# Expert up table read in pairs of neighbouring rows, gathers issued in order of release, and a third one-hot buffer, in a hybrid decoder layer

## The chip, the cores and the metric

The kernel runs on one core of a Trainium2 chip. The metric is the device time of one execution in microseconds (us); before the change it is 3395.63 us, the median of three runs (3392.81 to 3404.72).

## What is computed

One layer of a decoder for 1024 prompt tokens and 8 sample tokens, all in float32, with 1024 channels. Three gated branches (a convolution, windowed attention, attention to a memory) are summed and projected, and then comes a product-key expert mixer, which takes most of the time:

```python
q = (xb @ w_q).reshape(PEER_BLOCK, PEER_HEADS, 2, PEER_DK_HALF)
s = jnp.einsum('thcd,hcnd->thcn', q, keys)
sv, si = lax.top_k(s, PEER_TOPK)                       # 16 of 128 keys, twice per head
cand = sv[:, :, 0, :, None] + sv[:, :, 1, None, :]
cv, ci = lax.top_k(cand.reshape(...), PEER_TOPK)       # 16 of 256 pairs
eid = i0 * PEER_N_KEYS + i1                            # an expert is a pair of keys
u = w_down[eid]                                        # 128 experts per token
act = jax.nn.gelu(jnp.einsum('td,thkd->thk', xb, u), approximate=False)
out = jnp.einsum('thk,thkd->td', softmax(cv) * act, w_up[eid])
```

There are 16384 experts, so `w_down` and `w_up` are tables of 16384 rows of 4 KB (64 MB each). A token uses 128 of them.

## The kernel before, in words

**Tiles.** The tokens are cut into eight tiles of 128 (one token per partition) and the eight samples.

**Down side.** For each of the 1024 (tile, choice) pairs POOL issues one indirect DMA that gathers 128 rows of `w_down`, one per token, 512 KB in all (`fetch`, L1398), into one of a ring of row buffers; DVE multiplies it with the tokens and sums (`dot`, L2013, a "row" in what follows). The ring is a list of buffer places, each with a span of row numbers in which it may be used (`open_from`, `open_to`); from row 365 on a row's buffer is the one that was used five rows earlier, so five rows at most are on their way.

**Up side.** For the first seven tiles the sum over experts is a product with the whole table. PE scatters the 128 coefficients of each token into a dense 128 x 16384 matrix: DVE makes one-hot rows from the two key numbers (`one_hots`, L2037, four tokens for each compare, 32 compares a tile), ACT scales one of the two (`scaled`, L2315), PE multiplies them (`scatter`, L1463: "a scatter" is the product for four tokens), ACT copies the result out (`evacuate`, L2350). Then PE multiplies the dense matrix, in 128 blocks, with the table's blocks (`up_step`, L1660). SP reads a block of 512 KB (128 neighbouring rows, one for each partition) as one DMA (`fetch_up`, L1269) into one of four buffers; a block's DMA is issued once the step four blocks earlier has finished (`step_done`).

**Passes.** A stretch of 64 blocks is here called a pass, numbered 0 to 7. Pass n multiplies each block for tile n-1 (second half of its experts) and for tile n (first half), so that a block serves two tiles; pass 0 and pass 7 have one tile only. In the second half of passes 0 to 5 the 32 scatters of the next tile stand between the steps. The 32 scatters of tile 0 are woven between the last products ("items") ahead of pass 0. The last tile (tile 7) has no dense matrix: its 128 rows of `w_up` are gathered and added up on DVE (`up`, L2107).

**The order.** One list, `plan`, is made when the kernel is built, by a loop that simulates the engines with costs in a table and puts the next piece of DVE work down. DVE follows it word for word: rows, selections of keys and ids (the "keys" and "ids" entries, a pair of which makes one head), compares, sums. PE's order is fixed. Before the change POOL follows the same list: it issues the gathers of the rows up to the next "keys" entry, then waits until the head before is done and fetches that head's scores (`fetch_scores`, L1349), then the next rows.

## Time and profile before

| | before |
|---|---|
| median of three runs | 3395.63 us |
| profiled execution | 3393.68 us, of which 3391.9 us is the span that the profile shows |
| PE busy | 3106.5 us (92%) |
| DVE busy | 2512.9 us (74%) |
| DMA, mean over the span | 318 GB/s |
| granted TensorE clock, mean | 0.958 |

The profiled execution's time is 1.8 us more than its span, and 1.95 us less than the median. Windows of the trace (busy time of each engine between two times) cut the run into items (up to 1515 us), the eight passes (1515 to 3377 us) and the last normalisations. Shares of busy time say little here, since different engines set the pace in different stretches, so the waits of each stretch have to be read.

### The profile page before, as it was taken

The numbers are of one execution on the slowest core, as the hardware profiler recorded it, in microseconds if no ns is written. First come the engines' busy times: TensorE is split into PE (matmuls) and PEld (weight loads), VectorE is DVE, ScalarE is ACT, GpSimd is POOL, SyncE is SP. The second block draws the span as 40 slices with busy tenths as digits, with TensorE's granted clock in tenths as the row PEclk, the third lists the DMA queues.
The fourth block names the chain that finished last, engine by engine and source line by source line (L and its number), as shares of the span: only waits on it lengthen the run. The fifth ranks groups of instructions, "written<-read, shape, count | busy, mean of one in ns | idle before, by whom it ended". The sixth has DMA issues, their size and how long they took to land.

```text
span 3391.9 us, 33152 instructions
## 1 busy us (share of the span) xinstructions
PE 3106.5 (92%) x11349; PEld 1834.3 (54%) x11349; DVE 2512.9 (74%) x5082; ACT 779.3 (23%) x2062; POOL 1630.5 (48%) x1269
## 2 busy tenths in 40 slices
PE   8999798988888998778999999999999999997976
PEld 5677687857745754453545545545544545543322
DVE  2298435986877688878998888898888867646455
ACT  2001542312310003331503403403403403400000
POOL 0000002554055487862667656657756757644443
PEclk9999899999989799789999999999999999998999
DMA  3111457999398799999999999999999999899998
GB/s 131 44 36 65 151 194 252 336 365 333 129 342 313 296 401 379 340 336 345 388 393 393 355 376 366 359 389 381 356 389 369 351 399 377 321 411 393 408 410 328
DMA packets 326170, 1077.16 MB, mean 318 GB/s; under 512 B 40467, under 2 KB 73876, under 8 KB 325339
## 3 DMA queue, kind: packets, MB, share of 16 engines
q0 software_dynamic: 172416, 625.03, 48.1%
q1 hardware_dynamic: 119275, 428.87, 34.0%
q10 hardware_dynamic: 34312, 21.16, 2.0%
q8 instruction: 90, 1.47, 0.2%
q14 instruction: 77, 0.63, 0.1%
HBM read 1052.50 MB, written 23.94 MB: 317 GB/s over the span
## 4 chain that ended last, share of the span: by engine, by line
PE 37%; DMA 19%; DVE 14%; issue 10%; POOL 7%; ACT 1%; ACTq 0%; DVEq 0%; SPq 0%; POOLq 0%
PE psum L1660 22%; DMA arena<-in_w_down,arena 10%; DMA arena<-in_w_up,arena 7%; POOL arena L1398 6%; DVE arena L2013 5%; PE psum L1507 5%; PE psum L1463 4%; PE psum L1509 2%; PE psum L1636 1%; DMA arena<-in_w_q 1%; PE psum L1606 1%; DVE arena L2107 1%; DVE arena L2037 1%; DMA arena<-scratch_s 1%; PE psum L1523 1%
## 5 line engine op out<-in xcount | busy, mean ns | idle before, releaser
L1398 POOL DMA_INDIRECT arena<-in_w_down,arena x1024 | 1435.2, 1402 | 734.2 <-DVE arena L2013 484.9
L1660 PE MATMUL psum<-arena 128*128 128x512 f32 x3584 | 1603.8, 599 | 73.8 <-DMA arena<-in_w_up 70.4
L2013 DVE CUSTOM_DVE_ANT_0 arena<-arena 128x1024 f32<-128x1024 f32 x1024 | 1218.2, 1221 | 254.0 <-DMA arena<-in_w_down,arena 235.2
L1660 PEld LDWEIGHTS psum<-arena 128*128 128x128 f32 x3584 | 664.8, 192 | 869.6 <-issue 731.1
L1507 PE MATMUL psum<-arena 128*128 128x256 f32 (+2 forms) x1536 | 359.8, 388 | 16.1 <-DVE arena L1815 7.7
L2315 ACT ACTIVATE arena<-arena 128x128 f32<-128x128 f32 x896 | 286.1, 391 | 336.8 <-DVE arena L2037 317.5
L1463 PEld LDWEIGHTS psum<-arena 128*128 128x128 f32 x1792 | 244.3, 200 | 183.7 <-ACT arena L2315 104.3
L2037 DVE TENSOR_TENSOR arena<-constants,arena 128x1024 f32<-128x1024 f32 x224 | 273.4, 1222 | 88.0 <-PE psum L1463 72.9
L1507 PEld LDWEIGHTS psum<-arena 128*128 128x128 f32 x1536 | 266.4, 194 | 98.9 <-issue 15.5
L1463 PE MATMUL psum<-arena 128*128 128x128 f32 x1792 | 251.8, 286 | 71.7 <-ACT arena L2315 63.4
L2107 DVE SCALAR_TENSOR_TENSOR arena<-arena 128x1024 f32<-128x1024 f32 x128 | 164.4, 1284 | 133.1 <-DMA arena<-in_w_up,arena 130.8
L1349 POOL DMA_DIRECT2D arena<-scratch_s x64 | 37.6, 587 | 448.9 <-DMA scratch_s<-arena 214.6
L284 PE MATMUL psum<-arena 128*128 128x344 f32 x816 | 238.4, 455 | 3.0 <-DVE arena L324 3.0
L1398 POOL DMA_INDIRECT arena<-in_w_up,arena x128 | 130.0, 1016 | 170.7 <-DVE arena L2107 153.5
L2350 ACT ACTIVATE arena<-psum 128x128 f32<-128x128 f32 (+5 forms) x512 | 149.8, 352 | 265.4 <-PE psum L1463 210.6
L284 PEld LDWEIGHTS psum<-arena 128*128 128x128 f32 x816 | 155.7, 191 | 85.4 <-issue 5.7
L1509 PE MATMUL psum<-arena 128*128 128x256 f32 (+2 forms) x768 | 183.2, 381 | 0.0
L1335 POOL MEMSET constants<- 128x64 f32 x1 | 0.2, 152 | 346.5 <-POOLq L369 346.5
L345 DVE SCALAR_TENSOR_TENSOR arena<-arena,constants 128x1024 f32<-128x1024 f32 x120 | 154.2, 1285 | 4.3
L1636 PE MATMUL psum<-arena 128*128 128x256 f32 (+2 forms) x512 | 132.8, 422 | 23.6 <-DMA arena<-in_w_q 23.2
L1509 PEld LDWEIGHTS psum<-arena 128*128 128x128 f32 x768 | 132.8, 190 | 36.6 <-issue 0.3
L1636 PEld LDWEIGHTS psum<-arena 128*128 128x128 f32 x512 | 97.8, 214 | 54.5 <-DMA arena<-in_w_q 26.2
(317 smaller groups left out, 2078.5 us busy)
## 6 DMA issues: line engine op xcount, KB each, us to landing
arena<-in_w_up SPq DMA_DIRECT2D x512, 512.0 KB
arena<-in_w_gates SPq DMA_DIRECT2D x96, 768.0 KB
arena<-in_w_o SPq DMA_DIRECT2D x40, 512.0 KB
arena<-in_w_q SPq DMA_DIRECT2D x32, 512.0 KB
arena<-in_w_down,arena POOLq DMA_INDIRECT x1024
arena<-in_w_chunks SPq DMA_DIRECT2D x26, 512.0 KB, 3.4
arena<-scratch_s POOLq DMA_DIRECT2D x64, 128.0 KB
scratch_s<-arena ACTq DMA_DIRECT2D x11, 512.0 KB
```

The source lines that it names most:

```text
L284: mm = pe.matmul(psum[:, s + g, 0:GC], w[:, k, :], hT[:, k, g * GC:(g + 1) * GC], start=first, stop=last)
L345: link(dve.scalar_tensor_tensor(out=acc, in0=uT[:, c, t:t + SEQ], scalar=cw[:, c, t:t + 1], in1=acc, op0=ALU.mult, op1=ALU.add))
L1398: pool.indirect_dma_start(dst, None, table, bass.IndirectOffsetOnAxis(ap=idN[:, min(n, NT - 1) % 2, j:j + 1], axis=0)).then_inc(here, 16)
L1463: mm = pe.matmul(psum[:, 4 + g % 2, t * P:(t + 1) * P], pair[:, 1, t, :], pair[:, 0, t, :], start=True, stop=True)
L1507: pe.matmul(psum[:, b, 0:n], w[:, i, :], hT[:, i, cols], start=(i == 0), stop=(i == KD - 1))
L1509: mm = pe.matmul(psum[:, b + 1, 0:n], w[:, KD + c, :], branch[br][:, c, cols], start=(c == 0), stop=(c == NC - 1))
L1636: mm = pe.matmul(psum[:, b + h, 0:n], w[:, c, :], hT[:, c, cols], start=(c == 0), stop=(c == KD - 1))
L1660: mm = pe.matmul(psum[:, 2 * (m % 2) + h, :], coef_block(m, s % NKEYS), wup[s % WUPR][:, h * 512:(h + 1) * 512], start=first, stop=end)
L2013: dve.tensor_tensor_reduce(row, row, rowD[slot_of["x", n]], 1.0, 0.0, ALU.mult, ALU.add, dots[:, n % 3, j:j + 1]).then_inc(row_used, 1)
L2037: dve.tensor_tensor(out[:, g % 2], iota128.unsqueeze(1).unsqueeze(1).broadcast_to(full), ids[:, 0:2, BATCH * q:BATCH * (q + 1)].unsqueeze( ...
L2107: dve.scalar_tensor_tensor(out=acc, in0=row, scalar=dots[:, (NT - 1) % 3, u:u + 1], in1=acc if u else x1last, op0=ALU.mult, op1=ALU.add).t ...
L2315: ins = act.activation(buf[:, g % 2, 1, t, :], buf[:, g % 2, 1, t, :], ACT.Copy, scale=ids[:, 2, c:c + 1])
```

## The change

Four things are changed.

1. The up table is read in pairs: partition p gets the two neighbouring rows 128p + 2q and 128p + 2q + 1 (8 KB in one run), so a DMA moves 1 MB and there are 256 instead of 512. Partitions now lie 128 rows (512 KB) apart in the table. There are two buffers of 1 MB instead of four of 512 KB. A block is now "all experts with second key e" instead of "all with first key e", so the two operands of the scatter change places.
2. POOL has an order of its own, `pool_order`: row gathers, token tiles and score fetches are sorted by the time at which the plan's simulation has what each of them waits for.
3. Tile 0's one-hots have three buffers instead of two. The third stands where a row buffer (at 36864) was, which now closes at row 258 instead of 365.
4. The rule that places compares in the plan looks eight PE operations ahead instead of six for tile 0.

```diff
-        WUPR = 4
+        WUPR = 2
...
-            [310] + [258] * 2 + [50] * 2 + [238, 365]
+            [310] + [258] * 2 + [50] * 2 + [238, 258]
...
-        hot0 = at(33792, 2, 2, BATCH, P)
+        hot0 = [at(o, 2, BATCH, P) for o in (33792, 34816, 36864)]
+
+        def hot_of(g):
+            return hot0[g % 3] if g < NBATCH else hot[:, g % 2]
...
-        wup = [at(o, D) for o in (43008, 44032, 45056, 46144)]
+        wup = [at(43008 + 2 * D * i, 2, D) for i in range(WUPR)]
+        up_table = w_up.rearrange("(p e) d -> p e d", e=NKEYS)
...
-            if any(x[0:2] == ("scat", hot_next) for x in m.ops[m.at:m.at + (6 if hot_next < NBATCH else 1)]) and \
-                    m.done("turned", hot_next // NBATCH) and m.pe <= m.now + 6.5 and (hot_next < 2 or m.done("scated", hot_next - 2)):
+            if any(x[0:2] == ("scat", hot_next) for x in m.ops[m.at:m.at + (8 if hot_next < NBATCH else 1)]) and \
+                    m.done("turned", hot_next // NBATCH) and m.pe <= m.now + 6.5 and (hot_next < 3 or m.done("scated", hot_next - (3 if 2 < hot_next < NBATCH else 2))):
...
+        pool_order = [(m.fetch_at[f], 1, i, f) for i, f in enumerate(fetches)]
+        for k in range(HEADS * NT):
+            n, h = divmod(k, HEADS)
+            out_at = m.end["item", max(i for i in range(NI) if items[i] == ("score", n, h // 4))] + 5.0
+            pool_order.append((max(out_at, m.end["keys", (k - 1) // HEADS, (k - 1) % HEADS] if k else 0.0), 0, k, ("scores", n, h)))
+        for s in plan:
+            if s[0] in ("xprep", "sdown", "sup"):
+                pool_order.append((m.at_time[s], 2, 0, s))
+        pool_order = [x[3] for x in sorted(pool_order)]
...
-                def fetch_up(s):
-                    if s >= WUPR:
-                        sp.wait_ge(step_done, s - WUPR + 1)
-                    e = s % NKEYS
-                    sp.dma_start(wup[s % WUPR], w_up[e * NKEYS:(e + 1) * NKEYS, :])\
-                      .then_inc(wup_here[s % WUPR], 16)
+                def fetch_up(q):
+                    if q >= WUPR:
+                        sp.wait_ge(step_done, 2 * (q - WUPR + 1))
+                    e = 2 * q % NKEYS
+                    sp.dma_start(wup[q % WUPR], up_table[:, e:e + 2, :]).then_inc(wup_here[q % WUPR], 16)
...
-                for s in plan:
-                    if s[0] == "keys":
+                for s in pool_order:
+                    if s[0] == "scores":
                         fetch_scores(s[1], s[2])
-                    elif s[0] in ("dot", "up"):
-                        while fetched <= fetches.index(("row", row_index(s))):
-                            fetch(fetches[fetched])
-                            fetched += 1
+                    elif s[0] in ("row", "x"):
+                        fetch(s)
...
-                    if g >= 2:
-                        dve.wait_ge(scat_done, g - 1)
+                    if g >= (2 if n else 3):
+                        dve.wait_ge(scat_done, g - (1 if n else 2))
```

The plan's simulation then gives another order, so the change moves instructions on DVE and POOL. The first place is on DVE where tile 0's compares begin, among the last gated additions of the items (L1815 and L1818 before, L1826 and L1829 after). L2037 (L2048 after) is the compare, and each row's dot product is a pair of "ISA" entries at L2013 (L2024 after). Before:

```order
L1815 TENSOR_TENSOR arena<-arena,psum 128x392
L1818 TENSOR_TENSOR arena<-arena 128x3x128
L1818 TENSOR_TENSOR constants<-constants,arena 128x8
L2037 TENSOR_TENSOR arena<-constants,arena 128x1024 x2
L2013 ISA arena<-arena 128x1024
L2013 ISA arena 128x1
```

And after:

```order
L1826 TENSOR_TENSOR arena<-arena,psum 128x392
L1829 TENSOR_TENSOR arena<-arena 128x3x128
L1829 TENSOR_TENSOR constants<-constants,arena 128x8
L2048 TENSOR_TENSOR arena<-constants,arena 128x1024 x3
L2024 ISA arena<-arena 128x1024
L2024 ISA arena 128x1
```

Both stand after the same row; three compares instead of two now run ahead of the scatters. The second place is the 26th compare of tile 0 on DVE, in the middle of the woven scatters. L1973 to L1987 are the end of a head's selection. Before:

```order
L1973 MAX arena<-arena 128x8
L1975 TENSOR_TENSOR arena<-constants,arena 128x512
L1977 MAX arena<-arena 128x8
L1979 TENSOR_TENSOR arena<-arena 128x512
L1981 MAX_INDEX arena<-arena 128x8
L1983 TENSOR_REDUCE arena<-arena 128x2x16
L1985 MAX_INDEX arena<-arena 128x8
L1987 SCALAR_TENSOR_TENSOR arena<-arena 128x16
L2037 TENSOR_TENSOR arena<-constants,arena 128x1024
L2013 ISA arena<-arena 128x1024
```

And after, at the same compare (the last row):

```order
L2048 TENSOR_TENSOR arena<-constants,arena 128x1024
L2024 ISA arena<-arena 128x1024
L2024 ISA arena 128x1
L2024 ISA arena<-arena 128x1024
L2024 ISA arena 128x1
L2024 ISA arena<-arena 128x1024
L2024 ISA arena 128x1
L2024 ISA arena<-arena 128x1024
L2024 ISA arena 128x1
L2048 TENSOR_TENSOR arena<-constants,arena 128x1024
```

Before, three selection pieces stand between tile 0's first and last compare (10, 20 and 22 rows of the list, in all the keys of three heads and the ids of two); after, none does, and the first follows 19 rows after the 32nd compare. Counted in the whole lists, the rows (dot products) that DVE has ahead of some compares are: 32nd compare 371 before and 363 after; 64th 424 and 417; 96th 537 and 526; the last (224th) 983 and 971. The third place is the end of POOL's list. L1415 (L1426 after) are the eight gathers of `w_down` for the samples, which wait for the end of pass 5, L1421 (L1432) those of `w_up`. Before:

```order
L1392 DMA arena<-scratch_xn 128x1024
L1398 DMA arena<-in_w_down,arena 128x1024 x94
L1415 DMA arena<-in_w_down,constants 128x1024 x8
L1398 DMA arena<-in_w_down,arena 128x1024 x38
L1398 DMA arena<-in_w_up,arena 128x1024 x34
L1421 DMA arena<-in_w_up,constants 128x1024 x8
L1398 DMA arena<-in_w_up,arena 128x1024 x94
```

And after:

```order
L1406 DMA arena<-scratch_xn 128x1024
L1412 DMA arena<-in_w_down,arena 128x1024 x88
L1426 DMA arena<-in_w_down,constants 128x1024 x8
L1412 DMA arena<-in_w_down,arena 128x1024 x44
L1412 DMA arena<-in_w_up,arena 128x1024 x26
L1432 DMA arena<-in_w_up,constants 128x1024 x8
L1412 DMA arena<-in_w_up,arena 128x1024 x102
```

The samples' gathers, with their wait, stand after row 986 (1024 - 38) before and after row 980 (1024 - 44) now.

## Rows read from the trace of the kernel before

**Rows 1.** Window ahead of pass 0: busy us (x instructions), clock, DMA share, GB/s.

```profile
1300.00:1515.00 215.00, 164.90 (x672) 99.00 (x672) 183.79 (x333) 81.09 (x277) 163.38 (x109) 0.84 0.94 342
```

**Rows 2.** The same for passes 0 to 7: PE, PEld, DVE, ACT, POOL.

```profile
1515.00:1688.00 173.00, 149.25 (x516) 79.36 (x517) 154.21 (x390) 62.47 (x197) 74.17 (x57) 0.95 0.98 374
1688.00:1938.00 250.00, 250.00 (x772) 126.57 (x772) 218.30 (x479) 65.46 (x198) 171.52 (x123) 1.00 0.99 379
1938.00:2195.00 257.00, 251.79 (x772) 127.50 (x771) 224.09 (x511) 66.49 (x202) 160.44 (x119) 0.99 0.97 367
2195.00:2448.00 253.00, 249.59 (x773) 125.94 (x772) 221.41 (x491) 64.30 (x199) 171.09 (x121) 1.00 0.99 379
2448.00:2704.00 256.00, 250.15 (x771) 126.99 (x770) 218.76 (x492) 66.25 (x200) 170.41 (x121) 0.99 0.97 370
2704.00:2953.00 249.00, 249.00 (x775) 126.45 (x774) 182.36 (x287) 68.44 (x202) 152.23 (x107) 1.00 0.97 368
2953.00:3193.00 240.00, 222.52 (x512) 98.09 (x511) 122.55 (x155) 5.02 (x9) 112.42 (x109) 0.96 1.00 394
3193.00:3377.00 184.00, 142.01 (x289) 47.78 (x287) 102.70 (x81) 2.95 (x5) 73.90 (x73) 0.98 1.01 399
```

**Rows 3.** Chain that ended last, two neighbouring steps of pass 1: start us, us, what.

```profile
1803.70 3.44 PE psum L1660 x8
1808.03 3.44 PE psum L1660 x8
```

**Rows 4.** Waits of PE's weight loads, 1700 to 2953 us: us, times, longest.

```profile
PEld psum L1660 <- DMA arena<-in_w_up: 2.6, 2, 2.1
```

**Rows 5.** Waits of PE's weight loads, 3193 to 3377 us (pass 7).

```profile
PEld psum L1660 <- DMA arena<-in_w_up: 88.5, 58, 4.0
```

**Rows 6.** DMA queues, 3250 to 3350 us: packets, MB, share of 16 engines.

```profile
DMA packets 11244, 40.99 MB, mean 410 GB/s; under 512 B 1240, under 2 KB 1240, under 8 KB 11243
q0 software_dynamic: 5661, 20.61, 51.7%
q1 hardware_dynamic: 5582, 20.37, 50.9%
```

**Rows 7.** Windows of L1398 (gathers) on POOL, pass 1.

```profile
1688.00:1938.00 250.00, 166.62 (x114) 1.00 0.99 379
```

**Rows 8.** Windows of L2013 on DVE, pass 1 (two records for each row).

```profile
1688.00:1938.00 250.00, 133.36 (x224) 1.00 0.99 379
```

**Rows 9.** Waits of PE's weight loads, 1190 to 1515 us.

```profile
PEld psum L1463 <- ACT arena L2315: 44.5, 14, 8.4
```

**Rows 10.** Timeline of DVE, then of PE: start us, us, what [idle before <-releaser].

```profile
1314.39 0.29 DVE L1892 MAX8 arena<-arena 128x8 f32<-128x128 f32 x1
...
1316.74 1.21 DVE L2037 TENSOR_TENSOR arena<-constants,arena 128x1024 f32<-128x1024 f32 x1
...
1319.03 2.08 PE L1463 MATMUL psum<-arena 128*128 128x128 f32 x8 [5.33 <-ACT arena L2315]
```

**Rows 11.** Waits of DVE, 1190 to 1515 us.

```profile
DVE arena L2013 <- DMA arena<-in_w_down,arena: 35.6, 33, 4.1
```

**Rows 12.** DMA, issues with median us to landing.

```profile
arena<-in_w_chunks SPq DMA_DIRECT2D x26, 512.0 KB, 3.4
```

**Rows 13.** DMA, 3 to 9 us, when only reads of 8 KB runs (token matrix) move.

```profile
DMA packets 339, 2.53 MB, mean 422 GB/s; under 512 B 32, under 2 KB 32, under 8 KB 32
```

**Rows 14.** DMA queues, 640.95 to 643.6 us: gate weights (6 KB runs, q1) beside gathers (4 KB, q0).

```profile
q1 hardware_dynamic: 117, 0.68, 62.4%
q0 software_dynamic: 121, 0.42, 40.1%
```

**Rows 15.** Timeline of POOL at the samples' gathers.

```profile
2938.28 1.68 POOL L1398 DMA_INDIRECT arena<-in_w_down,arena  x1 [0.60 <-DVE arena L2013]
2958.43 0.94 POOL L1415 DMA_INDIRECT arena<-in_w_down,constants  x1 [18.48 <-PE psum L1660]
```

**Rows 16.** Windows, the end of pass 5.

```profile
2943.00:2960.00 17.00, 17.00 (x58) 8.95 (x57) 6.36 (x10) 7.15 (x15) 1.26 (x2) 1.00 0.51 144
```

More of the change, by code:

```diff
@@ L943, in ask_rows @@
                         return
-                    self.pool = max([self.pool, self.row_done.get(c - 1, 0.0)] + [self.end[x] for x in [needs] + joins])
+                    free = max([self.row_done.get(c - 1, 0.0)] + [self.end[x] for x in [needs] + joins])
+                    self.fetch_at[f] = max(free, self.fetch_at.get(fetches[self.next_fetch - 1], 0.0))
+                    self.pool = max(self.pool, free)
                     self.pool += 1.24 if f[0] == "row" else 0.3
@@ L1030, in put @@
                 self.now += 0.3 + group_cols(items[s[1]][3])[1] / 450.0 if s[0] == "evac" else COST[s[0]]
-                self.end[s] = self.now
+                self.end[s] = self.at_time[s] = self.now
             def done(self, *s):
@@ L1284, in _ @@
                 sp.wait_ge(xb_done, NX)
-                for s in range(WUPR - 1):
-                    fetch_up(s)
+                for q in range(WUPR - 1):
+                    fetch_up(q)
                 for i in range(2):
@@ L1290, in _ @@
                 sp.wait_ge(item_done, NI)
-                for s in range(WUPR - 1, HALF * (DENSE + 1)):
-                    fetch_up(s)
-                    k, i = s // HALF, s % HALF
+                for q in range(WUPR - 1, HALF * (DENSE + 1) // 2):
+                    fetch_up(q)
+                    k, i = 2 * q // HALF, 2 * q % HALF
                     if i == 40 and k == 1:
@@ L1455, in scatter @@
                     g = NBATCH * n + q
-                    pair = (hot if n else hot0)[:, g % 2]
+                    pair = hot_of(g)
                     pe.wait_ge(hot_ready, g + 1)
@@ L1660, in up_step @@
                         mm = pe.matmul(psum[:, 2 * (m % 2) + h, :], coef_block(m, s % NKEYS),
-                                       wup[s % WUPR][:, h * 512:(h + 1) * 512], start=first, stop=end)
+                                       wup[s // 2 % WUPR][:, s % 2, h * 512:(h + 1) * 512], start=first, stop=end)
                     return mm
                 def piece_here(s):
-                    pe.wait_ge(wup_here[s % WUPR], 16 * (s // WUPR + 1))
+                    pe.wait_ge(wup_here[s // 2 % WUPR], 16 * (s // 2 // WUPR + 1))
                 pe.wait_ge(copied, len(copy_no))
```

21 lines of the change are left out of this document (9 added, 12 removed).

## The prediction, made before the run

> **What bounds the kernel now.** I read the windows of the passes first, then each stretch's waits, then the DMA queues. PE is busy 92% of the span (the table above), which hides three regimes.
>
> Ahead of pass 0 PE works through the items with tile 0's scatters between them, busy 165 of the last 215 us [rows 1]. Its weight loads stood still for 44.5 us there, waiting for scaled one-hots [rows 9]. One of those waits can be followed: DVE selects a head's keys from 1314.39, makes the compare only at 1316.74, and PE, 5.33 us idle, starts the scatter at 1319.03 [rows 10]. A fixed list puts a selection ahead of what PE needs. DVE itself waited 35.6 us there for gathered rows [rows 11].
>
> Passes 1 to 5 take 249 to 257 us, with PE busy nearly throughout and the clock at 0.99 to 1.00, that is 2.4 GHz [rows 2]. A step of eight products takes 3.44 us, and 4.33 us with a scatter [rows 3]. 64 x 3.44 + 32 x 0.89 = 249 us, so PE sets the pace. It waited 2.6 us in all for the table [rows 4]. DMA is near its limit too (0.97 to 0.99), and beside 64 blocks it brings some 113 rows a pass [rows 7].
>
> Passes 0, 6 and 7 belong to the DMA. From 2953 to 3377 us (424 us, "the tail") it is busy at 1.00 and 1.01 [rows 2], and PE waited 88.5 us for the table in pass 7 [rows 5]. At its limit it moves 410 GB/s, and packet counts of both queues are equal [rows 6]: a block and a row together take 1.049 MB / 410 GB/s = 2.56 us. The tail holds 38 + 128 gathered rows, 128 blocks, 16 gathers and 8 broadcasts for the samples and some five transfers of results: 323 halves of a megabyte (0.524 MB), 1.28 us each, 413 us of the 424.
>
> So before pass 0 DVE's order decides, in passes 1 to 5 PE, in the tail the bytes that are left.
>
> **The change, part by part.**
>
> *The DVE order ahead of pass 0.* By the 32nd compare DVE has 8 rows fewer behind it, and the selections (keys of three heads, ids of two, about 2.4 heads) come later. A row costs 133.36 / 112 = 1.19 us [rows 8]. For a head I take what is left of DVE's 218.3 us in pass 1 [rows 2] after 133.4 us of rows and 32 compares at 1.21 us [rows 10]: 46 us for eight heads, 5.8 us at most. So 8 x 1.19 + 2.4 x 5.8 = 23 us less stand ahead of the last compare. PE can't gain more than the 44.5 us that it waited [rows 9], nor less than nothing. The third buffer lets a compare run one scatter earlier; that pays within the same 44.5 us, and I don't count it twice. I take -22.
>
> *The row buffer that closes at 258.* Between rows 258 and 365 there is one buffer less for rows: five or six on their way instead of six or seven. The DMA is 0.94 busy there [rows 1] and queueing makes up most of a gather's latency, so fewer in flight mostly wait less. Bounds: nothing, or DVE's 35.6 us of waiting [rows 11] doubled. Nearer to nothing: +4. Items together: -18.
>
> *Pass 0.* The pair's DMA has 8 KB packets. A queue with larger packets shares one for one by packets [rows 14]: 117 of 6 KB beside 121 of 4 KB, so the larger get the larger share (62% to 40%). With 8 KB beside 4 KB the table gets two thirds. A 512 KB load alone lands after 3.4 us [rows 12], of which 1.28 us is data, so 2.1 us is fixed. At 418 GB/s, between the rates of the two packet sizes [rows 6, 13], a pair then lands after 1.049 MB / (0.667 x 418) = 3.8 us plus 2.1 = 5.9 us. With two buffers and 3.44 us of products for a pair of one tile, a pair takes (5.9 + 3.44) / 2 = 4.7 us instead of 2 x 2.56 = 5.1. That would be 32 x 0.4 = 14 us, but DVE is busy 154 of 173 us in that pass [rows 2] and now also has the postponed selections. Bounds 0 and -14; I take -3.
>
> *Passes 1 to 5.* The change to 1 MB also takes lead away. Before, a block's DMA was issued three steps (10.3 us) ahead of its use; now a pair's is issued when the pair before the last is done, two steps, 6.9 us, ahead. 5.9 us fits with 1.0 us to spare, and where a scatter stands between steps with 2.8 us. So 0. What is queued behind a late pair is everything: PE's scatters, so ACT's copies and DVE's next compares. Of the 20 us by which these passes exceed 5 x 249 [rows 2] none is counted as gained.
>
> *POOL's order.* Of the release order the trace prices one place. POOL stopped 18.48 us at the samples' gathers, waiting for the end of pass 5 [rows 15], and DMA fell to 0.51 [rows 16]. DVE had all 986 rows behind it by then. Now the wait comes after row 980. PE still ends pass 5 on its own pace, so six rows more remain for the tail. Elsewhere the orders differ by a few rows around a score fetch, which its buffer's release hides either way: 0, bounds -10 and +10.
>
> *The tail.* Six rows more: 6 x 1.28 = +7.7 us. The table's 64 pairs move at the rate of 8 KB packets, 422 GB/s [rows 13], not 410 [rows 6]: 64 x 1.049 x (1/0.422 - 1/0.410) = -4.7 us. Together +3. PE's own minimum there (64 x 3.44 + 64 x 1.72 = 330 us and the samples' few products) stays under 424, so the bytes go on deciding.
>
> Sum: -18 - 3 + 0 + 3 = -18 us. Against the profiled execution's 3393.7 us that is 3375.7; this execution is 2 us under the median of the runs shown, so 3377.5, in round numbers 3377 us.
>
> One rule speaks against the change. Each partition's run now starts 512 KB after its neighbour's, and no load of the trace has such a pitch. The Trainium skill ("DMA: Bandwidth & Descriptors", section "Latency and other measured facts") warns of row pitches that are large powers of two: 207 GB/s per direction at 512 KiB against 214 when padded, and 103 at 4 MiB. By it the pairs would lose 3%, about what the larger packets give, and the sum would be -13 us; no run here shows it yet.
>
> **The rivals.**
>
> *No change that can be measured: the time comes back.* The 23 us are postponed, not removed. DVE's selections return in pass 0, where it is busy 154 of 173 us [rows 2], and the 12 rows by which DVE is behind at the last compare (971 against 983) cost 12 x 1.28 = 15 us in the tail if POOL's six do not soften it. With 4 to 8 us for the lost buffer, -22 turns into about 0: 3390 to 3400. For it: DVE 87% busy in passes 1 to 4. Against: PE paces these passes, so DVE can catch up 30 us in each.
>
> *Slower: two buffers are too few.* The place is PE's wait for the table in passes 1 to 5, now 2.6 us [rows 4]. It decides from a landing time of 6.9 us. If the queues shared by bytes instead of packets, a pair would take 5.1 + 2.1 = 7.2 us and be 0.3 us late in each of the 16 pairs of five passes that have no scatter: 80 x 0.3 = 24 us, enough to cancel the gain; at 8 us it is 88 us, and 16 more in the other halves. So 3400 to 3480. For it: DMA at 0.97 to 0.99, with little slack if one engine of sixteen lags. Against: the shares measured [rows 14].
>
> *Slower: the pitch.* If reads 512 KB apart got half the rate (what a queue has beside another one [rows 6]), a pair's data would take 3.8 us more of DMA time, land after 9.7 us, and each of 80 pairs would be 2.8 us late, the others 1.0: over 300 us, and the tail some 160 us longer: 3800 and more. Against: nothing in the trace, for nothing has this pitch. The skill's page named above puts the loss at 3% for this pitch and at a half only from 4 MiB.
>
> **How the numbers follow.** Forecast case (a gain of 11 to 50 us, 3345 to 3385): 0.58. Its own range is that, from PE's whole wait regained with pass 0's 14 us, down to a third of it. No change (3385 to 3406): 0.22. Two buffers too few: 0.14. Pitch: 0.05. The last 0.01 is a postponed selection that costs more than it gave. What a measurement of this kernel can tell from no change is about 0.3%, 10 us. Faster 0.58, same 0.22, slower 0.20. The range 3345 to 3405 leaves out the late buffers and the pitch.
>
> **What would show each step.** In the changed profile pass 0 should start near 1497 us with PE's wait for one-hots at 20 to 25 us instead of 44.5. Passes 1 to 5 should still take 249 to 257 us with PE's wait for the table under 10 us in all; over 20 us there means the two buffers. Queue 1's packets should be 8 KB, and the tail should move 410 to 422 GB/s and last about 427 us; under 400 GB/s means the pitch. Before the samples' gathers POOL should stop about as long as now. The prediction is wrong if pass 1 starts no earlier than 1688 us (the selections came back), or if a pass exceeds 262 us.

## The result, and the profile after

The kernel is slower: 3467.6 us median of 4 runs (3462.3 to 3479.8) against 3394.5 us for the kernel before on the same chip, a ratio of 1.0212 with a 95% interval of 1.0176 to 1.0247. The profiled execution has a span of 3463.6 us, 71.7 us above the 3391.9 us of before, at the same mean clock (0.96).

The windows of passes 0 to 7 in the kernel after answer to [rows 2]: length, then busy us of PE, PEld, DVE, ACT and POOL with their instructions, clock, DMA share, GB/s.

```profile
1499.00:1690.00 191.00, 151.57 (x515) 79.86 (x515) 151.51 (x391) 64.18 (x198) 71.43 (x58) 0.96 0.90 340
1690.00:1948.50 258.50, 251.28 (x769) 125.22 (x770) 226.04 (x526) 64.27 (x196) 165.21 (x120) 1.00 0.94 358
1948.50:2215.00 266.50, 253.95 (x775) 126.07 (x774) 221.40 (x499) 66.81 (x199) 166.09 (x118) 0.99 0.95 354
2215.00:2471.50 256.50, 251.00 (x773) 125.45 (x772) 217.18 (x475) 68.40 (x201) 179.01 (x121) 1.00 0.98 374
2471.50:2731.00 259.50, 251.53 (x774) 125.33 (x774) 216.56 (x477) 68.50 (x201) 174.27 (x119) 1.00 0.95 362
2731.00:2991.50 260.50, 251.75 (x773) 125.07 (x772) 195.19 (x353) 68.52 (x201) 169.37 (x115) 1.00 0.94 362
2991.50:3246.00 254.50, 229.12 (x516) 96.08 (x514) 134.35 (x177) 5.08 (x9) 133.87 (x113) 0.98 0.97 389
3246.00:3455.00 209.00, 152.90 (x288) 59.39 (x288) 109.98 (x89) 5.62 (x10) 87.53 (x75) 0.84 0.89 355
```

Pass 0 begins 16 us earlier than before, and from there everything is lost: pass 0 takes 191 us instead of 173 (+18), passes 1 to 5 take 1301.5 instead of 1265 (+36.5), passes 6 and 7 take 463.5 instead of 424 (+39.5). What follows pass 7 is 6 us shorter. -16 + 18 + 36.5 + 39.5 - 6 = 72 us. In passes 1 to 5 PE's busy time is nearly as before (1259.5 us in all, 1250.5 before); its idle time is new. The DMA share has fallen (0.94 to 0.98 in passes 1 to 5, where it was 0.97 to 0.99, and 0.89 in pass 7, where it was 1.01), so the transfers wait for buffers.

Waits of PE's weight loads in the kernel after (us, times, longest), ahead of pass 0, in passes 1 to 5 and in pass 7; the first answers to [rows 9], the others to [rows 4, 5].

```profile
PEld psum L1474 <- ACT arena L2326: 27.0, 12, 8.7
...
PEld psum L1671 <- DMA arena<-in_w_up: 87.8, 66, 3.2
...
PEld psum L1671 <- DMA arena<-in_w_up: 71.5, 18, 6.1
```

The wait for one-hots has shrunk from 44.5 to 27.0 us. The wait for the table in passes 1 to 5 has grown from 2.6 to 87.8 us. Not all of it is lost, because a weight load can wait while PE still works on earlier products. PE's own wait for the table there, which is lost, was 1.3 us and is now:

```profile
PE psum L1671 <- DMA arena<-in_w_up: 41.2, 44, 2.3
```

A piece of the chain of waits in pass 2 shows what the wait is (start us, us, what):

```profile
1956.17 0.04 issue
1956.21 7.15 PE psum L1671 x16
1963.36 0.02 issue
1963.38 8.74 DMA arena<-in_w_up
1972.12 0.04 issue
1972.17 7.15 PE psum L1671 x16
```

PE finishes the 16 products of a pair (two tiles) at 1963.36. That frees its buffer, and the next pair for that buffer can be used 8.74 us later. The other buffer holds 6.88 us of work, so PE stands still. Two pairs take 15.96 us instead of 13.76: each is 1.1 us late. Neighbouring pieces are 8.07, 8.24 and 9.13 us. The prediction had 5.9 us here. The chains of passes 1 to 5 have 35 such waits, 6.9 to 10.0 us long, 8.3 us in the mean. (A chain shows only pairs that came late.)

The DMA queues show what the time goes into. Three stretches of the piece of 8.07 us (from 1948.10, 1951.10 and 1954.10 on) have each queue's packets, MB and share of the engines. For 3 us there are only gathers (q0); then the table (q1) has 75% for 3 us and gets 0.94 MB; its last 0.11 MB take 2 us more:

```profile
q0 software_dynamic: 334, 1.21, 102.3%
...
q1 hardware_dynamic: 116, 0.94, 75.3%
q0 software_dynamic: 97, 0.33, 28.2%
...
q0 software_dynamic: 28, 0.11, 26.4%
q1 hardware_dynamic: 28, 0.11, 12.6%
```

Over all 35 waits the table's share of the engines' time is 4, 10 and 26% in the first three microseconds, 60, 75 and 58% in the next three, and 38 and 12% after that. What holds up the first and the last packets wasn't followed.

In passes 0 and 7 a pair serves one tile, eight products. The chain in pass 7:

```profile
3307.46 5.41 PE psum L1671 x8
3312.88 0.02 issue
3312.89 7.64 DMA arena<-in_w_up
3320.54 0.04 issue
3320.58 5.41 PE psum L1671 x8
```

Windows over the eight products that stand at the head of that piece; the clock is the third number from the end:

```profile
3307.40:3309.40 2.00, 1.94 (x3) 0.97 (x4) 1.28 (x1) 0.00 (x0) 0.20 (x1) 0.60 1.01 414
3309.40:3311.40 2.00, 2.00 (x3) 0.67 (x2) 0.27 (x1) 0.00 (x0) 0.74 (x1) 0.55 1.03 416
3311.40:3313.40 2.00, 2.00 (x6) 0.95 (x5) 1.96 (x2) 0.00 (x0) 0.71 (x1) 1.00 1.00 399
```

And one weight load early in it and one late, from the timeline (idle time before them in brackets):

```profile
3308.18 0.34 PEld L1671 LDWEIGHTS psum<-arena 128*128 128x128 f32 x1 [0.43 <-issue]
...
3311.84 0.19 PEld L1671 LDWEIGHTS psum<-arena 128*128 128x128 f32 x1 [0.24 <-issue]
```

Two pairs go by in 7.64 + 5.41 = 13.1 us, 6.5 us a pair, where 4.7 was predicted. Besides the landing there is a second loss: PE stood still for 4.67 us before this pair, and in the next 4 us the granted clock is 0.55 to 0.60 in the mean, so mostly at the lower level of 1.2 GHz. The first eight products take 5.41 us instead of 3.44, and a weight load 340 ns instead of 190. Before, the clock in this pass was 0.98 [rows 2]; now it is 0.84.

So the last work to end is now PE's, not the gathers'. The page's chain of the kernel after, by engine and line:

```profile
PE 48%; DMA 23%; issue 8%; DVE 7%; POOL 2%; ACT 1%; another core or an unknown queue 1%; SPq 0%; DVEq 0%; POOLq 0%
PE psum L1671 34%; DMA arena<-in_w_up 18%; PE psum L1474 4%; PE psum L1518 4%; DMA arena<-in_w_down,arena 3%; DVE arena L2024 2%; POOL arena L1412 2%; PE psum L1520 2%; PE psum L1647 1%; DMA arena<-in_w_q 1%; PE psum L1617 1%; PE psum L1534
```

The table's DMA is 18% of that chain. The gathers of `w_up` for the last rows, which ended the run before, don't appear among its lines.

### The profile page after: what moved, and what is told of

Read it like the earlier page. It is cut to its first block, busy times and chain, and to the rows that moved or that the text cites. A ratio compares the mean times of both kernels' runs of the same rounds, so it can differ in the third digit from the quotient of the medians.

```text
span 3463.6 us, 32898 instructions
## 1 busy us (share of the span) xinstructions
PE 3127.2 (90%) x11349; PEld 1828.7 (53%) x11349; DVE 2513.0 (73%) x5082; ACT 786.6 (23%) x2064; POOL 1669.1 (48%) x1269
## 4 chain that ended last, share of the span: by engine, by line
PE 48%; DMA 23%; issue 8%; DVE 7%; POOL 2%; ACT 1%; another core or an unknown queue 1%; SPq 0%; DVEq 0%; POOLq 0%
PE psum L1671 34%; DMA arena<-in_w_up 18%; PE psum L1474 4%; PE psum L1518 4%; DMA arena<-in_w_down,arena 3%; DVE arena L2024 2%; POOL arena L1412 2%; PE psum L1520 2%; PE psum L1647 1%; DMA arena<-in_w_q 1%; PE psum L1617 1%; PE psum L1534 1%; DMA arena<-in_w_gates 0%; ACT arena L2296 0%
## 5 line engine op out<-in xcount | busy, mean ns | idle before, releaser
L1671 PE MATMUL psum<-arena 128*128 128x512 f32 x3584 | 1636.3, 607 | 163.7 <-DMA arena<-in_w_up 160.0
L1412 POOL DMA_INDIRECT arena<-in_w_down,arena x1024 | 1452.7, 1419 | 670.3 <-DVE arena L2024 421.0
L2024 DVE CUSTOM_DVE_ANT_0 arena<-arena 128x1024 f32<-128x1024 f32 x1024 | 1214.5, 1222 | 206.0 <-DMA arena<-in_w_down,arena 195.6
L1671 PEld LDWEIGHTS psum<-arena 128*128 128x128 f32 x3584 | 670.1, 194 | 987.9 <-issue 730.4
L2048 DVE TENSOR_TENSOR arena<-constants,arena 128x1024 f32<-128x1024 f32 x224 | 274.0, 1227 | 143.9 <-PE psum L1474 100.0
L1518 PEld LDWEIGHTS psum<-arena 128*128 128x128 f32 x1536 | 265.4, 193 | 104.0 <-issue 18.4
L1474 PEld LDWEIGHTS psum<-arena 128*128 128x128 f32 x1792 | 236.6, 194 | 136.6 <-issue 73.8
L1474 PE MATMUL psum<-arena 128*128 128x128 f32 x1792 | 241.9, 279 | 28.0 <-ACT arena L2326 17.6
L1412 POOL DMA_INDIRECT arena<-in_w_up,arena x128 | 152.3, 1190 | 138.7 <-DVE arena L2118 108.2
L284 PEld LDWEIGHTS psum<-arena 128*128 128x128 f32 x816 | 155.7, 191 | 85.3 <-issue 5.6
L1520 PEld LDWEIGHTS psum<-arena 128*128 128x128 f32 x768 | 132.7, 190 | 37.7 <-issue 1.7
L1534 PE MATMUL psum<-arena 128*128 128x512 f32 x256 | 119.6, 614 | 18.2 <-DVEq L1836 9.6
```

The costliest lines, as they stand in the source:

```text
L284: mm = pe.matmul(psum[:, s + g, 0:GC], w[:, k, :], hT[:, k, g * GC:(g + 1) * GC], start=first, stop=last)
L1412: pool.indirect_dma_start(dst, None, table, bass.IndirectOffsetOnAxis(ap=idN[:, min(n, NT - 1) % 2, j:j + 1], axis=0)).then_inc(here, 16)
L1474: mm = pe.matmul(psum[:, 4 + g % 2, t * P:(t + 1) * P], pair[:, 0, t, :], pair[:, 1, t, :], start=True, stop=True)
L1518: pe.matmul(psum[:, b, 0:n], w[:, i, :], hT[:, i, cols], start=(i == 0), stop=(i == KD - 1))
L1520: mm = pe.matmul(psum[:, b + 1, 0:n], w[:, KD + c, :], branch[br][:, c, cols], start=(c == 0), stop=(c == NC - 1))
L1534: mm = pe.matmul(psum[0:tile_rows(t), bb + h, :], mergedT[:, t, i, :] if t < NT else mergedS[:, i, :], w[:, h * 512:(h + 1) * 512], start= ...
```

## The experiments

Ratios are to the kernel before, timed on the same chip, with 95% intervals. The table waits are PE's weight loads waiting for `w_up` in passes 1 to 5; PE's own waits, where given, are the part that is lost.

### Which part loses

**e1_old_table** is the kernel after with four buffers of 512 KB and the old reading; **e12_old_table_again** repeats it.

```diff
-        WUPR = 2
+        WUPR = 4
-        wup = [at(43008 + 2 * D * i, 2, D) for i in range(WUPR)]
+        wup = [at(o, D) for o in (43008, 44032, 45056, 46144)]
```

> The changed kernel with the table read as before: four buffers of 512 KB, contiguous blocks. POOL's release order, the third one-hot buffer and the new DVE order stay. Theory A (two buffers of 1 MB give PE too little lead, and that is all of the loss): pass 0 starts near 1499 us as in the changed kernel, passes 1 to 5 take 249 to 257 us again, PE waits under 10 us for the table in them, and the time is 3370 to 3385 us. Theory B (the new DVE or POOL order costs the time): passes stay at 255 to 265 us and the time is 3440 us or more. Theory C (the pitch): as A here.

Measured: 1.0024 (1.0006 to 1.0041), 3396.5 us; table wait 0.2 us; pass 0 starts at 1500. Nearly all of the loss is in the table's part. But theory A had 3370 to 3385 us here, and the rest of the change alone brings no gain; the runs below say why.

**e2_pairs_only** is the other way round: the kernel before with the pairs and two 1 MB buffers alone.

```diff
-        WUPR = 4
+        WUPR = 2
-                    sp.dma_start(wup[s % WUPR], w_up[e * NKEYS:(e + 1) * NKEYS, :])\
-                      .then_inc(wup_here[s % WUPR], 16)
+                    sp.dma_start(wup[q % WUPR], up_table[:, e:e + 2, :]).then_inc(wup_here[q % WUPR], 16)
```

> The kernel before with the table's part alone: pairs of rows, 8 KB runs, 1 MB transfers, two buffers, pitch 512 KB. A and C: 3465 to 3490 us, with PE waiting over 120 us for the table in all. B: 3385 to 3400 us.

Measured: 1.0348 (1.0327 to 1.0369), 3501.2 us, 11 us above the range of theories A and C; table wait 86.4 us in 59 waits, PE's own 45.6 us. The pairs alone cost more than the whole change.

### Pitch, size or lead

**e3_pitch_only** keeps four buffers of 512 KB, but partition p gets row 128p + e.

```diff
-                    sp.dma_start(wup[s % WUPR], w_up[e * NKEYS:(e + 1) * NKEYS, :])\
+                    sp.dma_start(wup[s % WUPR], up_table[:, e, :])\
```

> The kernel before with the layout alone: partition p reads row 128p + e, so partitions lie 512 KB apart, but runs are 4 KB, transfers 512 KB and buffers four. A: 3385 to 3405 us, as before. C (reads at a 512 KB pitch are slower): packets of queue 1 longer than the 159 ns that contiguous ones take, and 3430 us or more.

Measured: 0.9999 (0.9984 to 1.0014). DMA from 3250 to 3350 us in that kernel, beside [rows 6], in 40 slices and in all:

```profile
GB/s 410 410 408 410 413 408 410 411 408 410 410 410 411 406 418 418 415 408 410 411 406 408 411 408 408 413 410 408 413 406 411 410 406 413 408 410 413 388 292 306
DMA packets 11105, 40.40 MB, mean 404 GB/s; under 512 B 1245, under 2 KB 1245, under 8 KB 11104
```

The last three slices run out of gathers; the others are at 406 to 418 GB/s, where before moved 410. The table's own packets are the sharper test, which theory C named:

```profile
q1 hardware_dynamic: 4904, 17.83, 44.6%
```

44.6% of 16 engines for 100 us, over 4904 packets, is 146 ns for each, small packets included; before it was 146 ns too, from 50.9% and 5582 [rows 6]. So no cost of a pitch of 512 KB can be told here. The Trainium skill ("DMA: Bandwidth & Descriptors", section "Latency and other measured facts") has such a pitch 3% slower, for copies of rows of 16 KB between tensors in HBM. For these 4 KB reads beside gathers that is not seen.

**e4_pairs_no_pitch** is pairs and two buffers, but of 256 neighbouring rows, two for each partition, so with a pitch of 8 KB. Experts then meet the wrong coefficients: the output isn't the reference's, the work is.

```diff
-                    sp.dma_start(wup[q % WUPR], up_table[:, e:e + 2, :]).then_inc(wup_here[q % WUPR], 16)
+                    sp.dma_start(wup[q % WUPR], w_up[e * NKEYS:(e + 2) * NKEYS, :].rearrange("(p e) d -> p e d", e=2)).then_inc(wup_here[q % WUPR], 16)
```

(The diff is to e2.)

> As e2, but each 1 MB transfer reads 256 neighbouring rows, two for each partition, so the read is contiguous and has no pitch; each coefficient then meets another expert's row, so the output is not the reference's. A: the same time as e2 within 10 us. C: below e2 by 40 us or more.

Measured: 1.0327 (1.0298 to 1.0357), table wait 90.4 us: as with the pitch.

**e5_three_blocks** is the kernel before with three of its four 512 KB buffers. Its lead is two steps, as with the pairs, with half the bytes in each DMA.

```diff
-        WUPR = 4
+        WUPR = 3
```

> The kernel before with three buffers of 512 KB instead of four, so that a block is issued two steps (6.9 us) ahead of its use, as a pair is in the changed kernel, but brings half the bytes. Theory A1 (what is short is time for 1 MB to land in two steps; half as much lands in 5 to 6 us even beside gathers): 3385 to 3410 us, PE waiting under 25 us for the table in passes 1 to 5. Theory A2 (two steps of lead are too few whatever the size, because a gather in progress holds the queue up): 3430 us or more.

Measured: 1.0174 (1.0128 to 1.0221), 3451.6 us. Its table waits in passes 1 to 5, then PE's own wait in them:

```profile
PEld psum L1660 <- DMA arena<-in_w_up: 88.2, 97, 3.5
...
PE psum L1660 <- DMA arena<-in_w_up: 28.7, 34, 2.6
```

Two pieces of its chain of waits in pass 2:

```profile
1994.07 7.41 DMA arena<-in_w_up
...
2008.92 9.05 DMA arena<-in_w_up
```

So two steps of lead are too few for 512 KB as well (theory A2): the 32 waits in the chains of passes 1 to 5 are 6.9 to 9.8 us long, 7.6 us in the mean, where the pairs have 8.3. This doesn't show that the size of a transfer is without effect. With three buffers two blocks can be on their way at once, so the queue isn't relieved of half the bytes. In the second piece, of 9.05 us, it carried two blocks' worth:

```profile
q1 hardware_dynamic: 289, 1.08, 30.7%
```

With one block ahead of it, the prediction's own working gives 2.1 + 2 x 2.56 = 7.2 us, close to what was measured. And three small blocks cost less than two pairs: PE's own wait in passes 1 to 5 is 28.7 us against 45.6 in e2, and the whole 1.7% against 3.5%. The lead is one part of the loss. That a megabyte is released only as a whole may be the rest; it wasn't tested by itself. A single 512 KB block on its way, which would tell size from number, wasn't tried.

**e8_three_pairs** gives the kernel after a third 1 MB buffer. The room is taken from coefficients: of two groups of 32 blocks only 16 are kept and used twice (output not the reference's, a little less work for ACT).

```diff
-        WUPR = 2
+        WUPR = 3
-        wup = [at(43008 + 2 * D * i, 2, D) for i in range(WUPR)]
+        wup = [at(o, 2, D) for o in (43008, 45056, 38912)]
```

> The changed kernel with a third buffer of 1 MB. The room comes from leaving out work: in two of the eight coefficient places only the first 16 of 32 blocks are written, and are used twice, so the output is not the reference's; PE's work is the same, ACT copies out a little less. Theory A (the lead of two buffers is the whole loss): PE's wait for the table in passes 1 to 5 falls from 88 us to under 15, pass 0 and pass 7 take 165 and 185 us or less, and the time is 3370 to 3400 us. If the loss lies in 1 MB transfers or 8 KB packets as such (they hold up the gathers): 3440 us or more.

Measured: 1.0016 (0.9991 to 1.0042); no table wait in passes 1 to 5. DMA queues from 3200 to 3300 us:

```profile
DMA packets 8123, 41.66 MB, mean 417 GB/s; under 512 B 902, under 2 KB 902, under 8 KB 5179
q1 hardware_dynamic: 3597, 25.14, 60.6%
q0 software_dynamic: 4523, 16.47, 41.2%
```

With enough pairs in flight the table does get the larger share, 60.6% to 41.2%, and the rate is 417 GB/s. The rate is the prediction's 418; the share is 0.60 of the bytes where it had two thirds, and the packets don't go one for one (3597 to 4523). Theory A's 3370 to 3400 us was met with 3395. The loss is gone, but there is no gain over e1 (1.0024) either: 8 KB packets give nothing that can be told.

### The other parts

**e6_hot_only** is the kernel before with the third one-hot buffer, the look-ahead of eight and DVE's new order; **e11_hot_again** repeats it.

```diff
-        hot0 = at(33792, 2, 2, BATCH, P)
+        hot0 = [at(o, 2, BATCH, P) for o in (33792, 34816, 36864)]
-            if any(x[0:2] == ("scat", hot_next) for x in m.ops[m.at:m.at + (6 if hot_next < NBATCH else 1)]) and \
+            if any(x[0:2] == ("scat", hot_next) for x in m.ops[m.at:m.at + (8 if hot_next < NBATCH else 1)]) and \
```

> The kernel before with the third one-hot buffer, the row buffer closed at 258 and the look-ahead of eight alone, so with the new DVE order; the table and POOL's way of following the plan are those of before. Theory D (the start of pass 0 comes 10 to 20 us earlier, and DVE's 12 missing rows give it back in the tail): 3380 to 3395 us on this scale of before at about 3387. Theory E (POOL's release order is what costs e1 its 8 us): clearly below e1, 3370 to 3380 us.

Measured: 0.9972 (0.995 to 0.9994), 3380.0 us, on the border between theories D and E. The wait for one-hots falls to 22.8 us and pass 0 starts at 1481. Passes 6 and 7 with what follows them, in this kernel:

```profile
2920.00:3375.00 455.00, 363.85 (x800) 145.64 (x798) 246.39 (x268) 11.97 (x22) 194.09 (x194) 0.94 0.98 385
```

The same window of the kernel before:

```profile
2953.00:3390.00 437.00, 364.53 (x800) 145.88 (x798) 231.82 (x244) 12.07 (x22) 186.31 (x182) 0.96 0.98 387
```

Pass 6 starts 33 us earlier, and 18 of them are given back: POOL has 12 operations more left there (194 against 182). At 1.28 us a row, 12 rows are 15 us. This is the prediction's "the time comes back" in small.

**e7_pool_only** is the kernel before with POOL's release order.

```diff
-                for s in plan:
-                    if s[0] == "keys":
+                for s in pool_order:
+                    if s[0] == "scores":
```

> The kernel before with POOL's release order alone, everything else as before. D: no change, 3380 to 3393 us. E: 3395 us or more.

Measured: 0.9983 (0.9963 to 1.0003), not to be told from nothing, so by itself the order doesn't cost what theory E had. Pass 0 starts 7 us later in it than before (1522.8 against 1515.3).

**e9_pairs_hot** and **e10_pairs_pool** are the pairs with one of the other parts each. Against the kernel after, e9 has GpSimd's loop over the plan back, and e10 the old one-hots and look-ahead:

```diff
-                for s in pool_order:
-                    if s[0] == "scores":
+                for s in plan:
+                    if s[0] == "keys":
```

```diff
-        hot0 = [at(o, 2, BATCH, P) for o in (33792, 34816, 36864)]
+        hot0 = at(33792, 2, 2, BATCH, P)
```

> The kernel after with one thing put back: GpSimd issues its fetches in the order of the plan, as before. So: pairs in two 1 MB buffers, and the third one-hot buffer with VectorE's new order. Question: which of the two other parts gives back the 1.3% by which the kernel after (1.021) is faster than the pairs alone (1.035). Theory H (the one-hot part gives it: alone it measured 0.9972, and it starts pass 0 earlier): this run stands near 1.021 to 1.025 to the kernel before, its span 3460 to 3480. Theory O (the fetch order gives it: beside two buffers a gather issued late or early moves the landing of a pair): this run stands near the pairs alone, 1.030 to 1.035, span 3490 or more.

> The kernel before with the pairs in two 1 MB buffers and GpSimd's fetch order by release; one-hot buffers and VectorE's order as before. Theory H: it stands with the pairs alone, 1.031 to 1.036, and pass 0 starts at 1505 to 1520. Theory O: it stands near the kernel after, 1.020 to 1.026. Whatever the order, both theories expect the waits for the table in passes 1 to 6 to stay at 80 us or more, since the lead is still two steps.

Measured: 1.026 (1.0226 to 1.0294) and 1.0264 (1.0234 to 1.0295). Neither theory holds: each part takes about 0.8% off the pairs alone (1.0348), both together 1.3% (1.0212), though alone they give 0.3% and 0.2%. These ratios come from three chips, and repeats of one kernel on two chips differed by up to 0.3% (e1 and e12), so the sizes are rough. Table waits in passes 1 to 5 are 93.9 and 86.9 us, as in all kernels with two buffers. e10's profiled execution is 22 us above its median, so its stretches are not used. Why the release order gives something beside the pairs stays open.

> The third one-hot buffer and VectorE's new order alone, a second time, now beside the version that also has the new fetch order on the same chip. Theory 1 (it is a gain of a quarter of a per cent): 0.995 to 0.999 to the kernel before. Theory 2 (the first value was chance): 0.999 to 1.001.

> The kernel after with the old reading of the table (four buffers of 512 KB), a second time: third one-hot buffer, VectorE's order and the new fetch order. Theory P (the new fetch order takes back what the one-hot part gains): 1.000 to 1.004, above the run without the fetch order by 0.3% or more. Theory Q (the fetch order does nothing, and the difference between the first two measurements, 1.0024 and 0.9972, was that between chips or runs): both versions within 0.2% of each other.

Measured side by side: 0.9977 (0.9957 to 0.9997) and 0.9995 (0.9972 to 1.0019). The one-hot part alone is a gain of a quarter of a per cent, twice. Is the release order beside it free? The two ratios are 0.2% apart, which is theory Q's limit, but the first measurements of the two, 1.0024 (e1) and 0.9972 (e6), were 0.5% apart with the same sign, and the traces side with theory P. Passes 1 to 5 take 1276 and 1275 us with the release order (e1, e12), and 1259 and 1258 without it (e6, e11). In these passes DVE waits for a head's scores, with the order (e12) and without it (e11):

```profile
DVE arena L1960 <- DMA arena<-scratch_s: 20.6, 4, 5.4
...
DVE arena L1963 <- DMA arena<-scratch_s: 1.3, 2, 0.7
```

The other pair has 21.9 and 1.1 us, and PE's weight loads wait 13 to 19 us more for scaled one-hots. So beside the one-hot part the release order brings score fetches late. What comes after pass 5 is 6 to 8 us shorter with it, which gives part of that back. Of the versions with the whole computation, e6 and its repeat e11 have the lowest ratios; e7 (0.9983) can't be told from them.

### Why a table transfer lands late

Here the theory was contention with the gathers (C) against something in the issue itself (D). A first try halved the gathers by their rows. From the second tile on a gather fetches 64 rows into 64 partitions, once its buffer has been filled whole. The rest keeps old data, and the dot adds where it multiplied, in the kernel after (g1) and before (g2).

```diff
-                        pool.indirect_dma_start(dst, None, table, bass.IndirectOffsetOnAxis(
-                            ap=idN[:, min(n, NT - 1) % 2, j:j + 1], axis=0)).then_inc(here, 16)
+                        some = slice(0, 64 if n and fill[f] > 1 else P)
+                        pool.indirect_dma_start(dst[some], None, table, bass.IndirectOffsetOnAxis(
+                            ap=idN[some, min(n, NT - 1) % 2, j:j + 1], axis=0)).then_inc(here, 16)
```

> The kernel after, but from the second token tile on a gather of expert rows fetches 64 of its 128 rows, once its buffer has been filled whole (the other partitions keep old data, and the dot adds where it multiplied, so that old data stays finite: the output is not the reference's). The instructions, their sizes on VectorE and TensorE and the two 1 MB buffers stay; q0's bytes in the passes are half. Theory C (a pair lands late because its packets share the 16 engines with the gathers' packets): the waits for the table in passes 1 to 6 fall from 134 us to under 30, a pass takes 240 to 248 us where the kernel after has 253 to 265, and the first of pass 7 likewise; its time then comes within 10 us of g2's. Theory D (a pair lands late because of its issue: SyncE's queue, the release, the 8 KB packets): the waits stay at 100 us or more and g1 stays 45 us or more above g2.

> The kernel before with the same halved gathers and the same changed dot (output not the reference's); four buffers of 512 KB. It is the control: no waits for the table in passes 1 to 6 as before. Theory C: a pass of 240 to 250 us, nearly as before or a little less, and an end that is sooner where the gathers were its bound, 3300 to 3390 in all. Theory D expects the same of this one; what tells them apart is g1's distance from it.

Measured: 1.0586 (1.0532 to 1.064) and 1.0503 (1.047 to 1.0537). Half the gathered bytes made both kernels slower by 5 to 6%. The queues of g2 from 2300 to 2400 us:

```profile
DMA packets 6646, 22.97 MB, mean 230 GB/s; under 512 B 1048, under 2 KB 1048, under 8 KB 6642
q1 hardware_dynamic: 3474, 12.65, 49.2%
q0 software_dynamic: 3168, 10.26, 49.1%
```

The engines are full at 230 GB/s. The competition was not taken away, so this pair says nothing on C or D; the control, in which the table now waits 124.7 us, showed that.

The second try halves each row: 2 KB for each of 128 partitions (half rows of the table; output not the reference's), in the kernel after (h1) and before (h2), with the same dot.

```diff
+                        halves = table.rearrange("r (a d) -> (r a) d", a=2)
+                        some = slice(0, D // 2 if n and fill[f] > 1 else D)
+                        pool.indirect_dma_start(dst[:, some], None, halves if n and fill[f] > 1 else table, bass.IndirectOffsetOnAxis(
```

> The kernel after, but from the second token tile on, once its buffer has been filled whole, a gather fetches 2 KB instead of 4 KB for each of its 128 rows (half rows of the table; the other columns keep old data, and the dot adds where it multiplied: the output is not the reference's). The two 1 MB buffers and all instructions on the compute engines stay. Theory C (a pair lands late because its packets share the 16 engines with the gathers' packets): if the engines now are no longer full, the waits for the table in passes 1 to 6 fall from 134 us to under 30, and h1 comes within 15 us of h2. Theory D (a pair lands late because of its issue, the release or its 8 KB packets): the waits stay at 100 us or more, and h1 stands 45 us or more above h2. If the engines stay full although half the bytes are gathered, the run tells nothing again.

> The control: the kernel before with the same halved rows and the same changed dot (output not the reference's), four buffers of 512 KB. Theory C and D both expect no waits for the table in passes 1 to 6, passes of 238 to 252 us, and 3290 to 3370 in all; the DMA engines below 90% busy there. What tells the theories apart is h1's distance from it.

Measured: 0.9895 (0.9849 to 0.9941) for h1, 0.974 (0.9699 to 0.9781) for h2. The window of pass 1 in h1:

```profile
1647.00:1897.00 250.00, 249.32 (x772) 126.05 (x771) 226.54 (x531) 64.67 (x198) 176.88 (x120) 1.00 0.75 257
```

Its table waits in passes 1 to 5:

```profile
PEld psum L1673 <- DMA arena<-in_w_up: 29.4, 33, 3.5
```

The window of pass 1 in h2:

```profile
1656.00:1906.00 250.00, 250.00 (x770) 126.59 (x770) 217.39 (x483) 65.46 (x197) 183.08 (x123) 0.99 0.80 259
```

With the DMA 0.75 busy instead of 0.94 the same two 1 MB buffers nearly suffice: a pass of the pairs takes 250 us, the wait falls from 87.8 to 29.4 us, and the page of h1 gives 5.6 us from a pair's issue to its landing (h2: 4.8 us for 512 KB, at 0.80 busy). PE's own wait falls from 41.2 to 8.7 us. So in passes 1 to 5 most of it is contention (C). But h1 stays 49 us above h2, which is theory D's second sign (45 or more) and not C's (within 15). It begins pass 0 19 us earlier and loses 10 us in pass 0 (179 against 169), 13 in passes 1 to 5, 14 in pass 6 and 33 in pass 7 (186 against 153). Lighter gathers don't take that part away. Where a pair holds only 3.44 us of products, two buffers fall short even with light gathers. The kernel after shows it too, once its gathers have ended, in PE's timeline of the last two pairs:

```profile
3447.24 3.70 PE L1671 MATMUL psum<-arena 128*128 128x512 f32 x8 [1.37 <-DMA arena<-in_w_up]
3451.79 3.70 PE L1671 MATMUL psum<-arena 128*128 128x512 f32 x8 [0.86 <-DMA arena<-in_w_up]
```

A pair then takes 4.6 us, of which about 1 is waiting, with the DMA 0.54 busy (3402 to 3455 us).

## Why the prediction was wrong

**The step that failed** is that of passes 1 to 5: a pair lands after 5.9 us, which "fits with 1.0 us to spare", so 0. Where the chain waits, a freed buffer could be used again only after 6.9 to 10.0 us, 8.3 in the mean. I had worked the 5.9 out as 2.1 us fixed, from a 512 KB load that ran when the DMA was hardly used [rows 12], plus 3.8 us of data at the table's share. The share was nearly right (two thirds predicted; 75% in the middle of the piece above, 0.60 of the bytes in e8), and so was the decision point: late from 6.9 us. The fixed part was not fixed. In that piece 3 us pass before the table's first packet and 2 us over its last 0.11 MB, 5 us where I had 2.1. With the engines at 0.75 the pair takes 5.6 (h1), near what I had. An idle-time latency was used in a saturated stretch. Cost: +36.5 us, of which some 10 belong to the orders (e1's passes 1 to 5 take 1276 us, before's 1265).

**POOL's order, 0.** Beside the one-hot part it costs 17 us in passes 1 to 5 (e1, e12 against e6, e11), since score fetches come late; I had them hidden "either way". It also delays pass 0, by 19 and 4 us in these two pairs of traces and by 7 us in e7.

**Items, -18.** Pass 0 started at 1499, 16 us earlier, with the one-hot wait at 27.0 us (I had 20 to 25). The number is right in part by luck: the one-hot part alone gained 34 and 24 us there (pass 0 at 1481 in e6, at 1491 in e11), more than I had, and the release order took some of it back.

**Pass 0, -3.** It took 18 us more. My own formula, (landing + products) / 2 for a pair, was right in form; with the measured numbers of pass 7 it is (7.64 + 5.41) / 2 = 6.5 us against 4.7. Two terms were off: the landing by 1.7 us, and the products by 2.0 us, since the granted clock was down after the standstill.

**The tail, +3.** It came to +39.5 us up to PE's end. I held that "the bytes go on deciding" because PE's minimum was 330 us. The minimum leaves out that each pair waits for its buffer. 408 GB/s were still moved from 3246 to 3400 us, but the gathers took the share that the table could not use (59.9% against 42.2% from 3340 to 3390 us) and ended at about 3400, and PE was left alone with half-idle DMA. The six rows for POOL are too small to be seen beside it; POOL stopped at the samples' gathers for 9.95 us, where I had "about as long as now" (18.48).

**The pitch** costs nothing that can be told (e3, e4): the rival was rightly small. **The rival "two buffers are too few"** is what happened, for its stated reason (landing above 6.9 us), within its 3400 to 3480. Its cause was not the one I gave: while its packets flow the table has the larger share, but they start late and end late under load. I had looked for evidence on shares, and the row that I read as evidence against was about that. Its price was too high as well: with two buffers a late pair lengthens the lead of the next, so the lateness is paid once in two pairs (the 1.1 us above is half of 15.96 - 13.76). For 80 pairs, landing after 8.3 us, that gives 40 x 1.4 = 56 us, where the rival's own sum gives 112; PE waited 41.2. What spoke for it, a DMA at 0.97 to 0.99, stood in the rows [rows 2] and got too little weight.

**The rival "the time comes back"** is seen in e6, 18 of 33 us, and in e11, 18 of 28. Without the pairs the change would have been 1.0024 and 0.9995, so that rival's zone, not the forecast's -18 us, in part for its reason and in part by the release order.

**Left open:** why the table's packets start late and end late beside gathers, how much of the landing goes with the size of a transfer, and why the release order helps the pairs and hurts beside the one-hots. A full third pair buffer beside the whole computation was not tried, for want of room.

## What to carry to other kernels

Count the lead of a ring of buffers in time, not bytes: from the release of a buffer to the moment when its next use is due. Half as many buffers of twice the size took away one step of three here (10.3 to 6.9 us) and made the release coarser, and together that was 3.5% of the kernel (e2); the step alone was 1.7% (e5). For the landing take a number from the stretch in which the ring runs, under its load; if the trace has none, take away one buffer of the kernel as it is (e5), which measures at once how much lead is spare.

## What was not expected of the hardware

- Late loads beside gathers that keep the engines at 0.94 to 0.99 take 6.9 to 10.0 us from release to use for 1 MB (after) and 6.9 to 9.8 us for 512 KB with another block on its way (e5); 5.6 us from issue to landing for 1 MB at 0.75 busy (h1). In one of 8.07 us the table's queue carried nothing for the first 3 us.
- Gathers into 64 of 128 partitions kept the DMA engines full although they bring half the bytes: 230 GB/s at 49.2% + 49.1% (g2), with 10.26 MB in 3168 packets on q0. Halving the bytes of each row over all partitions does lighten it: 0.80 busy (h2). By which resource the half set of partitions is slow wasn't tried.
- PE waits of 4 to 5 us cost twice: after 4.67 us of standstill the granted clock was 0.55 to 0.60 for the next 4 us, and eight products took 5.41 us instead of 3.44.
